# Experts in half tiles: 64-row slices, two experts side by side, the second expert's weights copied to a fixed buffer

## The chip, the cores and the metric

One core of a Trainium2 chip runs the whole program in one launch. The metric is device time in microseconds (us), the median of the runs. The kernel before takes 1213.05 us (three runs, 1210.98 to 1215.25).

## What is computed

The reference is one inference step of a one-layer hybrid decoder for 1024 prompt tokens and 8 sample tokens, width 1024, all in float32. The change touches only the last part, a mixture of experts; of the reference this matters:

```python
def grouped_moe(h, w_router, b_router, w_gate, w_up, w_down):
    scores = jax.nn.sigmoid((t @ w_router).astype(jnp.float32))
    sel = scores + b_router.astype(jnp.float32)
    ...                       # best of 4 groups of 4 experts, then the top 2 in it
    combine = ...             # (T, 16), two entries per token, which add up to 1
    hg = jnp.einsum('td,edf->tef', t, w_gate)     # e = 16 experts, d = 1024, f = 256
    hu = jnp.einsum('td,edf->tef', t, w_up)
    act = jax.nn.silu(hg) * hu * combine[..., None].astype(t.dtype)
    out = jnp.einsum('tef,efd->td', act, w_down)
```

1032 tokens go to two experts each, which makes 2064 rows. With the inputs as drawn, the reference's router gives the 16 experts 101, 121, 137, 63, 316, 175, 149, 290, 32, 128, 124, 6, 125, 131, 38 and 128 of them. The parts before it (input projection, gated DeltaNet heads, S5 channel groups, output projection) and the final norm are the same in both kernels, but for where some of their buffers lie.

## The kernel before

The program is written out by hand for five engines, with semaphores between them. Its last section routes the tokens, runs the experts and ends with the final norm.

**Routing.** While the output projection runs (L2491), each block of 128 tokens is normed (`H2`), written to DRAM as `h2_d` by SyncE (L2368) and routed. GpSimd scatters each token's number into its expert's list in DRAM (`ids_d`, L2412). When all are counted, VectorE works out a table `slot_t`, which says for each slot (a tile of rows of one expert) the expert's weight buffer, how many loads must have landed, and where its list lies, and `exp_t`, which says after how many slots each expert is done.

**Slots.** A slot is 128 rows of one expert, and each expert has at least one. The counts above give 24 slots: 1, 1, 2, 1, 3, 2, 2, 3, 1, 1, 1, 1, 1, 2, 1 and 1. Each engine runs the slots in a hardware loop over pairs of them (`pairs`, L2060), the first pair written out ahead of the loop. For slot s the engines do this:

- GpSimd loads the list of 128 token numbers (L2095) and gathers the rows of `h2_d` by it (L2102).
- TensorE transposes the rows, 8 times 128x128 (L2137). VectorE copies them out of PSUM in two halves (L2226, L2228) into `xT`.
- TensorE multiplies them with the gate and up weights, which lie beside each other as 512 columns: 8 matmuls over the 8 blocks of 128 channels (L2173). I call this gate-up.
- ScalarE makes the silu (L2209), VectorE the product with the up half (L2240).
- TensorE transposes the two halves of that (L2143), VectorE copies them out (L2249), and TensorE multiplies with the down weights, 4 matmuls of 512 columns (L2155). I call this down.
- ScalarE copies the result out of PSUM in two halves (L2194, L2195) and starts its write to `ys_d` (L2198).

TensorE's order is gate-up of slot s, activation transposes of slot s-1, row transposes of slot s+1, down of slot s-1, and so on.

**Weights.** Gate and up of one expert are 2 MB (`wgu`, which lies in `hT`, two buffers), down is 1 MB (`wdn` in `y1T`, two buffers). SyncE loads both for experts 0 and 1 ahead of the slots. For expert e from 2 on (`moe_sync`, L2081) it waits for the gate-up of the last slot of expert e-2, issues gate and up (L2009), waits for the down of that slot, issues down (L2012), and goes on to e+1. The down of a slot comes on TensorE only after the next slot's gate-up.

**After the slots.** GpSimd gathers the two result rows of each token from `ys_d` (L2273), TensorE adds them with their weights (L2291), and VectorE and ScalarE do the residual, the norm and the output. The last expert's rows must be in DRAM first (`y_done`).

The loop's frame, which the change replaces:

Of the kernel before, what the change touches and what calls it, by code (L numbers as in the profile page):

```python
# [11 lines left out]
ALU = mybir.AluOpType  # L12
# [21 lines left out]
LAGS = 8  # L34
NCH = SEQ // LAGS
# [29 lines left out]
def emit(nc, A, O, marks):  # L65
# [11 lines left out]
    with ctx:  # L77
# [7 lines left out]
        hT = sb("hT", [P, KD, T])  # L85
# [73 lines left out]
        w_ring = s2.enter_context(nc.sbuf_tensor("w_ring", [P, 2, KD, 512], F32))  # L159
# [36 lines left out]
        early = room(w_ring[:, 1].rearrange("p k n -> p (k n)"))  # L196
        crow, sq, vrow = early(9, D), early(P, D), early(117, P)
        ada_row, cP = early(P, 2, 512), early(P, KD, 32)
# [26 lines left out]
        SLOTS = 2 * T // P + EXPERTS  # L225
        ys_d = dram("ys_d", ((SLOTS + 4) * P, D))
        gate_land, conv_land, conv_out = sem("gate_land"), sem("conv_land"), sem("conv_out")
        pe, act, dve, pool = steps("s2_pe"), steps("s2_act"), steps("s2_dve"), steps("s2_pool")
        with nc.Block() as block:
            @block.sync  # L230
            def _(sp):
# [5 lines left out]
                sp.dma_start(crow[0:1, :], A["c_prompt"]).then_inc(cland, 16)  # L237
                sp.dma_start(crow[1:9, :], A["c_sample"]).then_inc(cland, 16)
# [72 lines left out]
            def _(t):  # L311
# [4 lines left out]
                for k in range(KD):  # L316
                    mm = t.transpose(ps[7][:, k * 9:k * 9 + 9], crow[:, k * P:(k + 1) * P], ident[0:9, 0:9])
# [191 lines left out]
            def _(a):  # L509
# [6 lines left out]
                act.did(a.activation(crow[:, :], crow[:, :], ACT.Silu), "silu_c")  # L516
                dve.wait(a, "clear_ss")

                def squares(i):
# [3 lines left out]
                    act.did(a.activation(sq[0:n, :], X[0:n, i, :], ACT.Square, accum_out=small[0:n, i:i + 1]), f"ss{i}")  # L523
# [483 lines left out]
        t3 = lambda name, shape: s3.enter_context(nc.sbuf_tensor(name, shape, F32))  # L1007
        egl = t3("egl", [P, NT, HEADS])
        W3 = t3("W3", [P, 3328])
        Y = t3("Y", [P, 2, HEADS, P])  # L1010
        XS = t3("XS", [P, 1024])
        Yd, Xd = t3("Yd", [P, HB, BL]), t3("Xd", [P, HB, BL])
        Sd = t3("Sd", [P, DEC, HEADS, P])
        dec = t3("dec", [P, 768])
# [9 lines left out]

        R = W3[:, 0:512].rearrange("p (h n) -> p h n", h=HEADS)
        D1 = W3[:, 512:1536].rearrange("p (b h n) -> p b h n", b=2, h=HEADS)
        egb = W3[:, 1536:2048].rearrange("p (h n) -> p h n", h=HEADS)
        knd, ud = W3[0:DEC, 2048:2560], W3[0:DEC, 2560:3072]

        r = W3[:, 0:512].rearrange("p (h n) -> p h n", h=HEADS)  # L1030
        u = W3[:, 512:1024].rearrange("p (h n) -> p h n", h=HEADS)
# [521 lines left out]
        def load_ada(sp, c):  # L1553
            sp.dma_start(ada_col[c % 2][:, :, :], w_ada[:, :, (4 + c) * 512:(5 + c) * 512]).then_inc(ada_col_land[c % 2], 16)
# [1268 lines left out]
```

## Time and profile before

| | us |
|---|---|
| runs (three) | 1215.25, 1213.05, 1210.98 |
| median | 1213.05 |
| span of the profiled execution, first to last instruction | 1212.9 |
| of it, up to the first gate-up | 843.75 |
| from there to the start of the last slot's gate-up | 285.9 |
| from there to the end of the last down | 22.75 |
| final stage | 60.5 |

The profiled execution's own time is given only as its span, which is 0.15 us under the median of the runs. In the rows, times are us from the start of the span unless marked ns. PE is TensorE's matmuls, PEld its weight loads (which overlap them), DVE is VectorE, ACT is ScalarE, POOL is GpSimd and SPq is SyncE's queue. In brackets behind a row stands how long its engine had been idle before it, and what released it. A float32 matmul shows as two records of PE and two of PEld, a transpose as one.

### The profile page before, as it was taken

To read this page: it belongs to the slowest core of one execution; us is meant where nothing else is said; L and a number is where in the kernel's file an instruction comes from. 1 tells how busy PE (TensorE), PEld (TensorE's weight loads), DVE (VectorE), ACT (ScalarE), POOL (GpSimd) and SP (SyncE) were. 2 spreads that over 40 slices of the span, in tenths; PEclk is the share of its full clock that TensorE was granted. 3 is DMA by queue.
4 is the path that set the end of the run, shared out by engine and by line. 5 is a ranking of instruction groups with operands and counts; after the bars stand their busy time and mean duration, and the time that the engine had idled before them with its cause. 6 is when DMAs were issued, how large, how long until landed. Compare 5 with 4: busy or idle time off the path is not lost. (4 is left out here: it accounts for less than half of the span.)

```text
span 1212.9 us, 15216 instructions
## 1 busy us (share of the span) xinstructions
PE 1082.3 (89%) x5092; PEld 649.4 (54%) x5093; DVE 555.6 (46%) x1290; ACT 311.3 (26%) x703; POOL 220.2 (18%) x368
## 2 busy tenths in 40 slices
PE   4899999899998899699987999983999999889876
PEld 4466666445877777578853444442444444444332
DVE  4134446774448556799614325666212121121138
ACT  6121221125113643322234233330011111111033
POOL 0100000384423443211010000222111111111060
PEclk9999999999998879799888999995999999999888
DMA  9595170120016000566373001223776756788273
GB/s 347 175 289 214 66 273 5 70 102 38 14 28 128 15 1 21 201 222 235 137 268 120 31 18 41 100 69 71 235 251 215 234 191 201 262 296 294 87 296 140
DMA packets 128048, 182.02 MB, mean 150 GB/s; under 512 B 37725, under 2 KB 81490, under 8 KB 127982
## 3 DMA queue, kind: packets, MB, share of 16 engines
q1 hardware_dynamic: 116988, 147.03, 36.5%
q0 software_dynamic: 7376, 21.59, 5.6%
q10 hardware_dynamic: 3626, 12.64, 2.6%
q8 instruction: 35, 0.57, 0.2%
q14 instruction: 23, 0.19, 0.1%
HBM read 131.69 MB, written 48.47 MB: 149 GB/s over the span
## 5 line engine op out<-in xcount | busy, mean ns | idle before, releaser
L2173 PE MATMUL bank<-hT,H 128*128 (+1 forms) x384 | 172.1, 601 | 10.0 <-DMA hT<-in_w_up 5.4
L367 PE MATMUL bank<-hT,w_ring 128*128 128x344 f32 x576 | 169.6, 456 | 3.8 <-ACT hT L551 3.8
L367 PEld LDWEIGHTS bank<-hT,w_ring 128*128 128x128 f32 x576 | 109.9, 192 | 61.9 <-issue 5.2
L2173 PEld LDWEIGHTS bank<-hT,H 128*128 128x128 f32 x384 | 72.5, 192 | 107.2 <-issue 105.2
L2240 DVE TENSOR_TENSOR H<-H,bank 128x256 f32<-128x256 f32 x24 | 10.1, 421 | 238.1 <-ACT H L2209 238.1
L452 PE MATMUL bank<-w_ring,hT 128*128 128x512 f32 x256 | 114.7, 605 | 4.3 <-ACT qkvT L579 4.3
L2491 PE MATMUL bank<-w_out,hT 128*128 128x512 f32 x256 | 116.8, 601 | 0.5 <-DVE hT L1949 0.5
L2155 PE MATMUL bank<-y1T,H 128*128 (+1 forms) x192 | 91.2, 619 | 10.7 <-DVE H L2249 7.9
L452 PEld LDWEIGHTS bank<-w_ring,hT 128*128 128x128 f32 x256 | 64.2, 255 | 50.5 <-issue 32.1
L2491 PEld LDWEIGHTS bank<-w_out,hT 128*128 128x128 f32 x256 | 46.3, 190 | 49.8 <-issue 47.2
L2155 PEld LDWEIGHTS bank<-y1T,H 128*128 128x128 f32 x192 | 35.4, 194 | 52.2 <-issue 51.8
L2209 ACT ACTIVATE H<-bank 128x256 f32<-128x256 f32 x24 | 9.2, 385 | 177.5 <-PE bank L2173 177.5
L2102 POOL DMA_INDIRECT H<-h_d,small_room x24 | 23.4, 977 | 124.9 <-DMA small_room<-ids_d 85.2
L911 DVE SCALAR_TENSOR_TENSOR qkvT<-pre,vecT,qkvT 128x1024 f32<-128x1024 f32 x36 | 46.0, 1279 | 0.0
L573 ACT ACTIVATE pre<-bank 128x344 f32<-128x344 f32 x36 | 13.9, 458 | 122.9 <-PE bank L367 122.9
L2194 ACT ACTIVATE H<-bank 128x512 f32<-128x512 f32 x24 | 14.3, 597 | 119.7 <-PE bank L2155 119.7
L2412 POOL DMA_INDIRECT ids_d<-small_room x18 | 18.1, 1004 | 133.3 <-DVE small_room L2665 119.8
L2137 PE MATMUL bank<-ident,H 128*128 128x128 f32 x200 | 26.9, 279 | 11.6 <-DMA H<-h_d,small_room 11.6
L2095 POOL DMA_DIRECT2D small_room<-ids_d x25 | 14.0, 558 | 126.6 <-issue 125.9
L2291 PE MATMUL bank<-w_out,hT 128*128 128x512 f32 (+1 forms) x56 | 27.3, 639 | 8.5 <-DMA w_out<-ys_d,pos 6.2
L904 DVE COPY tail<-pre 128x11 f32<-128x11 f32 x12 | 2.1, 173 | 71.1 <-ACT pre L573 71.1
L1894 PE MATMUL bank<-H,y1T 128*128 128x512 f32 (+1 forms) x72 | 33.5, 626 | 0.2 <-DMA H<-in_s_glu_b 0.2
(556 smaller groups left out, 1757.5 us busy)
## 6 DMA issues: line engine op xcount, KB each, us to landing
ys_d<-ZO SPq DMA_DIRECT2D x18, 1024.0 KB, 13.1
y1T<-in_w_down SPq DMA_DIRECT2D x16, 1024.0 KB, 5.5
hT<-in_w_gate SPq DMA_DIRECT2D x16, 1024.0 KB, 7.2
hT<-in_w_up SPq DMA_DIRECT2D x16, 1024.0 KB, 10.4
ys_d<-H ACTq DMA_DIRECT2D x24, 512.0 KB, 5.2
w_ring<-in_w_in SPq DMA_DIRECT2D x4, 2048.0 KB, 8.3
y1T<-in_w_ada SPq DMA_DIRECT2D x4, 2048.0 KB, 9.1
hT<-in_w_ada SPq DMA_DIRECT2D x4, 2048.0 KB, 14.2
```

The lines of the kernel that those rows point to most:

```text
L367: mm = t.matmul(ps[3 * (m % 2) + s][:, 0:SEG], w_ring[:, q % 2, k, (m % 4) * P:(m % 4 + 1) * P], hT[:, k, s * SEG:(s + 1) * SEG], start=(k ...
L452: mm = t.matmul(ps[b % 4][0:n, :], tok, w_ring[:, q % 2, k, :], start=(k == 0), stop=(k == KD - 1))
L911: dve.did(v.scalar_tensor_tensor(out=y, in0=pre[:, m % 2, i:i + SEQ], scalar=taps[i], in1=y, op0=ALU.mult, op1=ALU.add), f"conv{m}")
L1894: mm = t.matmul(ps[2 + i % 2][0:n, :], y1T[:, k, i * P:i * P + n], glu_w[:, k, :], start=(k == 0), stop=(k == 3))
L2102: g.indirect_dma_start(xin[p][:, :], None, h2_d, bass.IndirectOffsetOnAxis(ap=who[p][:, 0:1], axis=0)).then_inc(x_in[p], 16)
L2137: mm = t.transpose(ps[k // 4][:, (k % 4) * P:(k % 4 + 1) * P], xin[p][:, k * P:(k + 1) * P], ident[:, :])
L2155: mm = t.matmul(ps[5 + half_][:, :], aT[p][:, k, :], wdn[:, bass.ds(buf, 1), k, half_ * 512:(half_ + 1) * 512].rearrange("p o n -> p (o n) ...
L2173: mm = t.matmul(ps[2 + p][:, :], xT[p][:, k, :], wgu[:, bass.ds(buf, 1), k, :].rearrange("p o n -> p (o n)"), start=(k == 0), stop=(k == K ...
L2194: a.activation(yo[p][:, 0:512], ps[5][:, :], ACT.Copy).then_inc(y_half, 1)
L2291: mm = t.matmul(ps[(5, 2)[i % 2] + half_][:, :], diag[0:n, i % 2, j, :], ya[i % YA][0:n, j, half_ * 512:(half_ + 1) * 512], start=(j == 0) ...
L2412: g.indirect_dma_start(ids_d, bass.IndirectOffsetOnAxis(ap=spot[0:n, i, j:j + 1], axis=0), ids[0:n, i:i + 1], None).then_inc(scat, 16)
L2491: mm = t.matmul(ps[b][:, :], hT[:, k, i * P:(i + 1) * P], w_out[:, k, cols], start=(k == 0), stop=(k == KD - 1))
```

## The change

- A slot becomes a **tile** of two **slices** of 64 rows (`LANES = 2`, `SLICE = 64`). Each expert gets as many slices as its rows need (at least one, the first expert at least two), and consecutive slices share a tile, so a tile can hold two experts. The counts above give 2, 2, 3, 1, 5, 3, 3, 5, 1, 2, 2, 1, 2, 3, 1 and 2 slices, together 38, in 19 tiles. Tile 3 holds experts 2 and 3, tile 6 holds 4 and 5, tile 9 holds 6 and 7, tiles 12 to 14 hold 8 and 9, 9 and 10, 10 and 11, tile 17 holds 13 and 14; in the others both slices are of one expert.
- In gate-up and down each matmul becomes two, one per slice, with 64 stationary columns and its own half of the PSUM partitions, and the same 512 moving columns each from its own weights.
- The first slice's weights are addressed by a register, the second's lie in a fixed fourth buffer. Each tile copies them there, even where both slices are of one expert: of gate-up, ScalarE and VectorE copy 2048 elements per partition each, of down 1024 each.
- There are three weight buffers for loads instead of two (`BUFS = 3`). Expert 2's weights are loaded ahead of the tiles too, its down weights behind the decode rows' `h2_d` write, its gate and up weights right behind expert 1's. For expert e from 3 on SyncE waits for expert e-3.
- To make room, `hT` and the output weights lie in one tensor `hw` (a row of `hT` is no longer followed by the next), `y1T` and `Yt` in one tensor `yy`, and buffers of the earlier sections lie in pieces of `hw`.
- GpSimd waits for the loads of both slices and then signals `gu_ready` and `dn_ready`; the list of a tile is fetched by an indirect transfer.
- The loop is written out: 17 tiles always, then up to 8 more, each behind an `If`, and behind each the end of the section under another `If`.

The core of the diff:

```diff
@@ weights
-        wgu = hT[:, :, 0:SEQ].rearrange("p k (b n) -> p b k n", b=2)
-        wdn = y1T[:, :, :].rearrange("p k n -> p (k n)")[:, 0:4 * D].rearrange("p (b k n) -> p b k n", b=2, k=2)
+        BUFS = 3
+        wgu = hw[:, :, 0:(BUFS + 1) * 2 * FE].rearrange("p k (b n) -> p b k n", b=BUFS + 1)
+        wdn = yy[:, 0:(BUFS + 1) * 2 * D].rearrange("p (b k n) -> p b k n", b=BUFS + 1, k=2)
@@ the frame
+        def tiles(eng, body, tail):
+            for s in range(LEAST):
+                body(s)
+            used = eng.value_load(exp_t[0:1, EXPERTS - 1:EXPERTS], min_val=LEAST, max_val=MOST)
+            for s in range(LEAST, MOST + 1):
+                if s < MOST:
+                    with eng.If(used > s):
+                        body(s)
+                with eng.If(used == s):
+                    tail(s - 1)
@@ SyncE
         def moe_sync(sp):
             dve.wait(sp, "slots")
+            for e in range(BUFS, EXPERTS):
+                done = sp.value_load(exp_t[0:1, e - BUFS:e - BUFS + 1], min_val=1, max_val=MOST)
+                sp.wait_ge(gu_ps, done)
+                load_gate_up(sp, e)
+                sp.wait_ge(dn_ps, done)
+                load_down(sp, e)
@@ GpSimd
+            def weights(s, landed, first, unit, ready):
+                need = [g.value_load(slot_t[0:1, s, first + b:first + b + 1], ...) for b in range(BUFS)]
+                for b in range(BUFS):
+                    g.wait_ge(landed[b], need[b])
+                g.sem_inc(ready, 1)
+            def body(s):
+                rows_in(s + 1)
+                if s + 2 <= MOST:
+                    list_in(s + 2)
+                weights(s + 1, gu_in, 2, 32, gu_ready)
+                if s > 0:
+                    weights(s, dn_in, 5, 16, dn_ready)
@@ the copies (eng is ScalarE with n = 0, VectorE with n = 1)
+        def gate_up_copy(eng, copy, n, s):
+            b = second(eng, s)
...
+                eng.wait_ge(gu_ready, s)
+                eng.wait_ge(gu_ps, s)
+            copy(wgu[:, BUFS, 4 * n:4 * n + 4, :], wgu[:, bass.ds(b, 1), 4 * n:4 * n + 4, :].rearrange("p o k n -> p (o k) n")).then_inc(gu_two[n], 1)
@@ TensorE, gate-up (down likewise)
-                    for k in range(KD):
-                        mm = t.matmul(ps[2 + p][:, :], xT[p][:, k, :], wgu[:, bass.ds(buf, 1), k, :].rearrange("p o n -> p (o n)"),
-                                      start=(k == 0), stop=(k == KD - 1))
+                for k in range(KD):
+                    if k % 4 == 0:
+                        t.wait_ge(gu_two[k // 4], s + 1)
+                    for j in range(LANES):
+                        lane = slice(j * SLICE, (j + 1) * SLICE)
+                        mm = t.matmul(ps[2 + p][lane, :], xT[p][:, k, lane], wgu[:, bass.ds(bufs[j], 1), k, :].rearrange("p o n -> p (o n)"),
+                                      start=(k == 0), stop=(k == KD - 1))
@@ ScalarE
+            def body(s):
...
+                a.activation(sg[p][:, :], ps[2 + p][:, 0:FE], ACT.Silu).then_inc(silu_sb, 1)
+                gate_up_copy(a, copy, 0, s + 1)
+                if s > 0:
+                    out(s - 1)
+                down_copy(a, copy, 0, s)
@@ VectorE
+            def body(s):
...
+                    a_copy(s - 1)
+                gate_up_copy(v, v.tensor_copy, 1, s + 1)
+                x_copy(s + 1)
+                v.wait_ge(silu_sb, s + 1)
...
+                v.tensor_tensor(hh_[p][:, :], sg[p][:, :], ps[2 + p][:, FE:2 * FE], ALU.mult).then_inc(h_sb, 1)
+                down_copy(v, v.tensor_copy, 1, s)
@@ SyncE ahead of the tiles
+                    elif i == ORDER[8]:
+                        pe.wait(sp, f"mix{i}_1")
+                        load_gate_up(sp, 1)
+                        load_gate_up(sp, 2)
```

How this stands on TensorE, for one slot of the kernel before inside its loop (`hT` and `H` are weights and rows; each row of gate-up is one block of 128 channels):

```order
L2173 ISA [waits h_sb]
L2173 MATMUL bank<-hT,H 128x512
L2173 ISA
L2173 MATMUL bank<-hT,H 128x512
...
L2143 MATMUL bank<-ident,H 128x128 [waits h_sb]
L2143 MATMUL bank<-ident,H 128x128
L2133 ISA
L2137 MATMUL bank<-ident,H 128x128 [waits xT_sb,x_in1]
L2137 MATMUL bank<-ident,H 128x128 x7
```

and for one tile of the changed kernel, L2202 being gate-up and `hw` holding the weights:

```order
L2202 ISA [waits h_sb,gu_two_act,gu_ready,xT_sb]
L2202 MATMUL bank<-hw,H 64x512 x2
L2202 ISA
L2202 MATMUL bank<-hw,H 64x512 x2
L2202 ISA
...
L2185 MATMUL bank<-ident,H 128x128 [waits h_sb]
L2185 MATMUL bank<-ident,H 128x128
L2179 MATMUL bank<-ident,H 128x128 [waits xT_sb,x_in0]
L2179 MATMUL bank<-ident,H 128x128 x7
```

Each block of channels has two matmuls of 64 stationary columns in place of one of 128, and gate-up waits for the copies (`gu_two_act`, `gu_two_dve`) beside the rows. On VectorE one slot of the loop before was this:

```order
L2240 TENSOR_TENSOR H<-H,bank 128x256 [waits aT_ps]
L2248 REGISTER_ALU [waits aT_ps]
L2249 COPY H<-bank 128x256 [waits dn_ps]
L2223 REGISTER_ALU
L2226 COPY H<-bank 128x512 [waits gu_ps,xT_ps]
L2228 COPY H<-bank 128x512 [waits xT_half]
```

and one tile now is this:

```order
L2294 COPY H<-bank 128x256 [waits aT_ps]
L2146 TENSOR_LOAD slot_t
L2146 ISA x2
L2156 ISA [waits gu_ps,gu_ready]
L2156 COPY hw<-hw 128x4x512
L2286 COPY H<-bank 128x512 [waits gu_ps,xT_ps]
L2288 COPY H<-bank 128x512 [waits xT_half]
L2311 TENSOR_TENSOR H<-H,bank 128x256 [waits silu_sb]
L2146 TENSOR_LOAD slot_t
L2146 ISA x2
L2165 ISA [waits dn_ps,dn_ready]
L2165 COPY yy<-yy 128x1024
```

The copy of the transposed activations moved from behind the product to the front, the copy of the gate-up weights stands ahead of the two row copies, and the product and the copy of the down weights stand behind them.

## Rows read from the trace of the kernel before

**Rows 1.** The page: the span, and one group of instructions that runs once per slot.

```profile
span 1212.9 us, 15216 instructions
...
L2209 ACT ACTIVATE H<-bank 128x256 f32<-128x256 f32 x24 | 9.2, 385 | 177.5 <-PE bank L2173 177.5
```

**Rows 2.** Stages: us, busy (instructions) by engine, granted clock, DMA share, GB/s.

```profile
1038.50:1129.65 91.15, 82.97 (x239) 39.08 (x239) 14.35 (x28) 10.28 (x21) 10.72 (x14) 1.00 0.84 288
1129.65:1152.40 22.75, 18.29 (x46) 8.24 (x45) 2.48 (x5) 2.56 (x5) 0.00 (x0) 0.85 0.25 93
```

**Rows 3.** TensorE's timeline over one steady slot: start, us, what, count, idle before.

```profile
953.19 7.03 PE L2173 MATMUL bank<-hT,H 128*128 x16
960.05 0.38 PE L2143 MATMUL bank<-ident,H 128*128 128x128 f32 x2
960.27 1.04 PE L2137 MATMUL bank<-ident,H 128*128 128x128 f32 x8
961.57 3.69 PE L2155 MATMUL bank<-y1T,H 128*128 x8 [0.26 <-DVE H L2249]
...
965.37 7.13 PE L2173 MATMUL bank<-hT,H 128*128 x16
```

**Rows 4.** TensorE's timeline inside the output projection: the 32-column matmuls of the decode rows.

```profile
721.44 0.19 PEld L2491 LDWEIGHTS bank<-w_out,hT 128*128 128x128 f32 x1 [0.24 <-issue]
722.39 0.16 PEld L2494 LDWEIGHTS bank<-w_out,hT 128*32 128x32 f32 x8 [0.76 <-issue]
722.39 3.64 PE L2494 MATMUL bank<-w_out,hT 128*32 128x512 f32 x32
```

**Rows 5.** Groups by line: VectorE and ScalarE over 512 and 1024 elements from SBUF.

```profile
L743 DVE TENSOR_SCALAR ZO<-ZO,small 128x1024 f32<-128x1024 f32 x8 | 5.6, 749 | 0.1
L1943 DVE TENSOR_SCALAR Yt<-Yt,small 128x512 f32<-128x512 f32 x8 | 3.3, 483 | 0.1
L2316 ACT ACTIVATE hT<-X 128x1024 f32<-128x1024 f32 x8 | 8.5, 1057 | 26.7 <-DVE X L2337 26.7
```

**Rows 6.** Timeline of VectorE after a gate-up that ended at 1045.6.

```profile
1046.22 0.42 DVE L2240 TENSOR_TENSOR H<-H,bank 128x256 f32<-128x256 f32 x1 [10.36 <-ACT H L2209]
1046.56 0.42 DVE L2249 COPY H<-bank 128x256 f32<-128x256 f32 x1
1046.89 0.68 DVE L2226 COPY H<-bank 128x512 f32<-128x512 f32 x1
...
1047.61 0.69 DVE L2228 COPY H<-bank 128x512 f32<-128x512 f32 x1
```

**Rows 7.** TensorE's waits among the slots, then the timeline around one late load.

```profile
PE bank L2173 <- DMA hT<-in_w_up: 5.4, 2, 3.0
...
1038.40 0.37 SPq L2012 DMA_DIRECT2D y1T<-in_w_down  x1
...
1039.89 0.38 SPq L2009 DMA_DIRECT2D hT<-in_w_gate  x1
...
1053.83 7.13 PE L2173 MATMUL bank<-hT,H 128*128 x16 [3.02 <-DMA hT<-in_w_up]
```

**Rows 8.** Timeline from the list scatters to the second slot.

```profile
818.84 0.96 POOL L2412 DMA_INDIRECT ids_d<-small_room  x1 [0.30 <-issue]
826.42 0.60 POOL L2406 DMA_DIRECT2D small_room<-ids_d  x1 [6.63 <-DMA ids_d<-small_room]
...
840.27 1.97 PE L2137 MATMUL bank<-ident,H 128*128 128x128 f32 x8 [11.58 <-DMA H<-h_d,small_room]
843.75 9.02 PE L2173 MATMUL bank<-hT,H 128*128 128x512 f32 x16 [1.51 <-DVE H L2228]
...
855.47 7.13 PE L2173 MATMUL bank<-hT,H 128*128 x16 [1.82 <-DVE H L2228]
```

**Rows 9.** TensorE's timeline behind the loop: the last down, the final stage's first matmuls.

```profile
1146.36 6.18 PE L2155 MATMUL bank<-y1T,H 128*128 x8 [2.83 <-issue]
...
1164.40 9.11 PE L2291 MATMUL bank<-w_out,hT 128*128 128x512 f32 x16 [6.21 <-DMA w_out<-ys_d,pos]
```

More of the change, by code:

```diff
@@ L34 @@
 LAGS = 8
+LANES = 2
+SLICE = P // LANES
 NCH = SEQ // LAGS
@@ L2182, in tail @@
-            def tail(it, s):
-                act_transposes(1, s)
-                down(1, s)
-            transposes(0, 0, 0)
-            pairs(t, body, tail)
+                        for j in range(LANES):
+                            lane = slice(j * SLICE, (j + 1) * SLICE)
+                            mm = t.matmul(ps[5 + half_][lane, :], aT[s % 2][:, k, lane],
+                                          wdn[:, bass.ds(bufs[j], 1), k, half_ * 512:(half_ + 1) * 512].rearrange("p o n -> p (o n)"),
+                                          start=(k == 0), stop=(k == 1))
@@ new lines, in down, with tail @@
+                mm.then_inc(dn_ps, 1)
+            def body(s):
+                gate_up(s, buffers(s))
+                if s > 0:
+                    act_transposes(s - 1)
+                transposes(s + 1)
+                if s > 0:
+                    down(s - 1, buffers(s - 1))
+                elif s == 0:
+                    dve.wait(t, "slots")
+            def tail(s):
+                act_transposes(s)
+                down(s, buffers(s))
+            for j in range(LANES):
+                if j == 0:
+                    dve.wait(t, "el")
+                mm = t.matmul(ps[5][0:1, P + j * S2_:P + (j + 1) * S2_], ident[:, j * SLICE:j * SLICE + 1], el[:, :], start=True, stop=True)
@@ L2188, in moe_scalar, with out @@
+            pe.did(mm, "e_rows")
+            transposes(0)
+            tiles(t, body, tail)
         def moe_scalar(a):
-            def out(it, p, s):
+            def out(s):
+                p = s % 2
                 a.wait_ge(dn_ps, s + 1)
-                if not (isinstance(it, int) and it == 0):
-                    a.wait_ge(y_out[p], it * 16)
+                if s >= 2:
+                    a.wait_ge(y_out[p], 16 * (s // 2))
                 a.activation(yo[p][:, 0:512], ps[5][:, :], ACT.Copy).then_inc(y_half, 1)
@@ L2375, in _ @@
             def _(g):
+                for b in range(BUFS):
+                    g.sem_inc(gu_in[b], 1)
+                    g.sem_inc(dn_in[b], 1)
                 pool.did(g.tensor_copy(pick16[:, :], ident[:, 0:EXPERTS]))
```

500 lines of the change are left out of this document (245 added, 255 removed).

## The prediction, on record before the changed kernel ran

> **What bounds the kernel now.** I read the page first, then the windows by stage, then TensorE's timeline and waits among the slots. The span is 1212.9 us, and a group that runs once per slot counts 24 [rows 1], as the counts of rows per expert say. The first gate-up starts at 843.75 [rows 8], the last slot's at 1129.65 [rows 2], 23 steps in 285.9 us. In a steady slot TensorE has one idle time, 0.26 us ahead of down; from gate-up to gate-up it takes 965.37 - 953.19 = 12.18 us [rows 3]. So 23 steps come to 280.1, and 5.4 us of the rest are two waits for gate and up weights [rows 7]. The experts are bound by TensorE, slot by slot, and a slot costs the same however few of its 128 rows are used. In the last stretch of slots the DMA engines are busy for 0.84 of the time at 288 GB/s, TensorE for 83.0 of 91.2 us [rows 2]: the transfers are the next bound there.
>
> **What goes.** 24 slots become 19 tiles. The question is what a tile costs, and what late weights cost when each tile eats more of them.
>
> **A tile on TensorE.** Gate-up has 16 matmuls of 64 stationary columns in place of 8 of 128, with the same moving columns. The 16 records of a slot take 6.86 us from their start to the first transpose [rows 3], 0.43 us each. If the halves ran one after the other, a tile would need 32 times 0.43. The nearest row is a group of 16 matmuls with 32 stationary columns in four column groups and four different moving operands: 32 records in 3.64 us [rows 4], where one after the other they would take 13.8, so 3.8 of 4 ran at once. I take it that two halves run fully beside each other, and gate-up stays at 6.86 and down at 3.80 (961.57 to 965.37) [rows 3]. The Trainium skill (TensorE: Matmul & The Clock Gate, Part 3) gives 2.38 times for three column groups, 0.79 of the ideal. By that ratio gate-up and down would take 1.26 times as long; the trace of this kernel disagrees, with 3.8 of 4.
>
> Changing from 128 to 32 columns costs something: the weight load stands 0.95 us behind the one before it, not 0.43 [rows 4]. The load can't go beside the matmul ahead of it. Its matmul then waits some 0.25 us that it didn't before (the load of 0.16 and the gap; bounds 0 and 0.52). A tile has two such changes, out of gate-up into the transposes and back into down: 0.5 us. Against that the 0.26 us wait ahead of down goes, since VectorE now copies the transposed activations first. A tile: 6.86 + 1.26 (transposes) + 3.80 + 0.5 = 12.4 us. Bounds: 11.9 without cost for the changes, 13.0 with 0.52 each.
>
> **The copies.** VectorE handles 1024 float32 from SBUF in 749 ns and 512 in 483 [rows 5], 0.52 ns each; 2048 come to 1.28 us, 1024 to 0.75. ScalarE handles 1024 in 1057 and 256 in 385 [rows 5, 1], 0.875 ns each; 2048 come to 1.95 us, 1024 to 1.06. TensorE has 1.26 + 3.80 + 0.5 = 5.6 us between two gate-ups. In it VectorE does the activations' copy (0.42, after 0.4 of transposes), its weight copy (1.28) and the two row copies (1046.89 to 1048.30, 1.41 [rows 6]): 3.5 us. ScalarE does the silu (0.39) and its copy (1.95): 2.4. Both fit, and the down copies have a whole tile. Price 0 in the steady tile, hidden by TensorE's own 5.6 us. Even with VectorE at one element per 1.04 ns, twice the price, it is 4.8 and fits. The register loads for buffers and semaphores run on the sequencers ahead of their work, as they do now; 0.
>
> **Late weights.** The copies aren't hidden when a tile waits for its weights: then come GpSimd's signal (0.2, a guess), VectorE's copy and the row copies behind it (2.7) and a handover of 0.1, 3.0 us from landing to gate-up. Where does this happen? Before, gate of expert 10 was issued at 1039.89, as SyncE was held by the down of the slot before until 1038.4 and then needed 1.5 us, and gate-up began at 1053.83 [rows 7]: 13.9 us, less 0.2 is 13.7 from issue to both landed. Now from tile 12 on every tile needs one new expert. Let G be the start of gate-up of tile 13. Expert 11 waits for expert 8, long done, but SyncE is held by the down of tile 11, which ends at G. It issues at G + 1.5, lands at G + 15.2, gate-up of tile 14 starts at G + 18.2 and not at G + 12.4: 5.8 lost. Expert 12 is issued after the down of tile 12, at G + 13.8, and lands at G + 27.5, just in time for tile 15 (G + 30.6). Expert 13 waits for the down of tile 13, which came late with tile 14; issued at G + 32.1, it opens tile 16 at G + 48.8 and not at G + 43.0: 5.8 again. Experts 14 and 15 are issued soon after one another and are in time. So 11.6, say 12 us, where 5.4 stand now. Bounds: 0, if a load takes less than before, and 30, if five tiles wait for 5.9 each.
>
> **The start.** Four MB of weights are issued at 811 in place of two. The scatters of token numbers landed only 6.6 us after the last was issued [rows 8], and on that chain hangs the first gather, which ended TensorE's wait of 11.58 us at 840.27. With twice the bytes ahead of them I give it 3 us (0 to 7; the upper end is about the 6.6 once more). The first step from gate-up to gate-up was 11.72 (843.75 to 855.47); now VectorE copies weights behind gate-up (9.02 - 0.1, then 1.28, 1.41 and 0.3), 12.0.
>
> **The end and the rest.** Behind the last gate-up all is as before: 22.75 us to the end of the last down [rows 2], then the final stage. The new code has 11 skipped blocks there; I give it 0, as TensorE waits 6.21 us for gathered rows [rows 9] and would be late by that much before anyone notices. The moved buffers change strides, not amounts, in the earlier sections: 0, bounds -1 and +2.
>
> **Sum.** From the first gate-up before to the last tile's now: 3 + 12.0 + 17 times 12.4 (210.8) + 12 = 237.8, against 285.9. That is 48.1 less, and 1212.9 - 48.1 = 1164.8 by the profiled execution, whose span is 0.15 under the median. I forecast 1165 us.
>
> **Rivals.**
>
> *No load is late.* Three buffers and a request two tiles ahead would cover it, if SyncE's being held didn't count. Against: it counted twice before. Without the 12 us: 1153.
>
> *Weights bound the last tiles.* The stretch that moved 288 GB/s had one expert per slot like these, and DMA at 0.84 [rows 2]; a third buffer adds no bandwidth. If tiles 14 to 18 all wait 5.9, 30 in place of 12: 1183.
>
> *Skipped code.* Behind the loop TensorE stood for 2.83 us with nothing but its own sequencer to wait for [rows 9]. Now it must pass five unused tile bodies of code written out. If each costs 2.83, 14.2 less the cover of 6.2 is 8 us: 1173. The Trainium skill (Runtime: NRT & Kernel Launch, Instruction fetch mechanics) says that a taken branch to code outside the two pages held forces a fetch before execution goes on. No row here shows such a fetch by itself.
>
> *The halves don't overlap (slower).* Two column groups could do worse than four: each float32 matmul has two records that must follow one another in the same columns, and with only two groups nothing else may be ready. One after the other, the 12 blocks of gate-up and down cost 0.86 us more each, 19 times 12 times 0.86 = 196: 1361. It decides from 48.1 / 228 = 0.21 us per block: above 1.07 us for both halves, in place of 0.86, the kernel gets slower. The Trainium skill's ratio of 0.79, cited above, would give 1.09, and so 1217. For it speaks only that no row shows two groups at 512 columns; against it stand the 32 records in 3.64 us [rows 4].
>
> **How the numbers follow.** My forecast 0.60, no late load 0.09, weights bound 0.14, skipped code 0.10, halves not overlapping 0.07. The first four are faster, the last slower: faster 0.92, same 0.01, slower 0.07. Within 0.3% is what a measurement of this kernel can't tell from no change. The range takes in the first four with the bounds of a tile (17 times 0.5 down, 17 times 0.6 up) and of the start: from 1153 - 6 = 1147 to 1183 + 9 = 1192.
>
> **What would show it.** TensorE's timeline should have 19 gate-ups of about 6.9 us and starts 12.4 apart in the middle; 13 or more there means that column changes or copies cost more, 22 that the halves don't overlap. Waits in front of gate-up for copies of late weights should stand at tiles 14 and 16, some 6 us each, and nowhere before tile 12. The first gate-up should start near 847. TensorE's idle time after the last down, up to the first sum of gathered rows, should stay at 12 us; if it grows, the skipped code costs. I'm wrong if the middle step isn't within 11.9 to 13.0, or if the waits of the last seven tiles lie outside 0 to 30.

## The result, and the profile after

| | before | after |
|---|---|---|
| median, us | 1214.13 (1210.98 to 1215.25, 4 runs) | 1166.12 (1158.17 to 1167.80, 4 runs) |
| ratio, with 95% interval | 1 | 0.9594 (0.9563 to 0.9625) |
| profiled execution: span, us | 1212.9 | 1166.0 (its own time 1167.80) |
| mean granted clock of TensorE | 0.941 | 0.924 |

The changed kernel is 48 us faster, and 1165 was forecast. The spans differ by 46.9 us, and four stretches make that up:

| stretch | before | after | difference | forecast |
|---|---|---|---|---|
| start to the first gate-up | 843.75 | 849.88 | +6.1 | +3 |
| first gate-up to the last one | 285.9 | 229.9 | -56.0 | -51.1 |
| last gate-up to the end of the last down | 22.8 | 20.8 | -2.0 | 0 |
| from there to the end | 60.5 | 65.4 | +4.9 | 0 |

The total is right to 1 us. Its terms are not, and they cancelled by luck, as the rest of this document shows. The page of the changed kernel, first part and costliest groups (the columns are those of [rows 1]):

```profile
span 1166.0 us, 15446 instructions
...
L2202 PE MATMUL bank<-hw,H 128*64 (+1 forms) x608 | 141.0, 618 | 16.3 <-DVE H L2288 13.5
...
L2274 ACT ACTIVATE hw<-hw 128x2048 f32 (+1 forms) x20 | 38.2, 1911 | 39.3 <-DVE small_room L2336 18.9
...
L2156 DVE COPY hw<-hw 128x2048 f32 (+1 forms) x20 | 24.5, 1226 | 22.6 <-POOLq L2122 14.6
...
L2263 ACT ACTIVATE H<-bank 128x256 f32<-128x256 f32 x19 | 7.3, 385 | 75.1 <-PE bank L2202 75.1
```

The silu group, 24 in [rows 1], counts 19: the change does what it says. Gate-up's 608 records are 19 times 32. The weight copies took 1.23 us on VectorE and 1.91 on ScalarE, where 1.28 and 1.95 were worked out from [rows 5].

TensorE's timeline of one steady tile (start, length, line, operation, count, idle time before it), to be laid beside [rows 3]:

```profile
945.81 7.04 PE L2202 MATMUL bank<-hw,H 128*64 x32
952.78 0.44 PE L2185 MATMUL bank<-ident,H 128*128 128x128 f32 x2
953.05 1.04 PE L2179 MATMUL bank<-ident,H 128*128 128x128 f32 x8
954.02 3.65 PE L2220 MATMUL bank<-yy,H 128*64 x16
957.50 7.04 PE L2202 MATMUL bank<-hw,H 128*64 x32
```

From gate-up to the first transpose 32 records take 6.97 us. Sixteen records of 128 columns took 6.86. Two experts beside each other thus cost what one cost. The tile takes 957.50 - 945.81 = 11.69 us, where 12.4 was forecast and a slot had 12.18. The idle 0.26 us ahead of down is gone. [Rows 3] show one of two kinds of slot, which took turns in the kernel before: in the other, down waited 0.43 us, and the slot took 12.18 as well.

The stretch between the first gate-up and the last is 12.33 us for the first tile, 17 times 11.69 (198.8), and three lumps on top of these: 1.75 in the second tile, 8.6 in tile 14 and its follower, 8.4 in tile 16 and its. TensorE's waits from 800 to 1110 us (engine, line, what it waited for, total, times, longest):

```profile
PE bank L2202 <- DVE H L2288: 13.5, 3, 6.2
...
PE bank L2392 <- issue: 7.0, 1, 7.0
...
PE bank L2220 <- ACT yy L2274: 3.3, 1, 3.3
PE bank L2202 <- ACT hw L2274: 2.8, 1, 2.8
```

The first is mostly the two waits of tiles 14 and 16. The second and third come up below. The fourth is the second tile waiting for the copies of its weights, of which ScalarE's ended last. It lies in the first tile's 12.33 us; the 1.75 us of the second tile are its gate-up, 8.79 us long in place of 7.04. The timeline at the late loads, TensorE's rows first, then SyncE's and VectorE's that fall between them:

```profile
1004.28 7.04 PE L2202 MATMUL bank<-hw,H 128*64 x32
...
1022.34 9.32 PE L2202 MATMUL bank<-hw,H 128*64 x32 [6.20 <-DVE H L2288]
...
1036.31 7.04 PE L2202 MATMUL bank<-hw,H 128*64 x32
...
1054.00 8.85 PE L2202 MATMUL bank<-hw,H 128*64 x32 [5.83 <-DVE H L2288]
...
1004.49 0.37 SPq L2022 DMA_DIRECT2D yy<-in_w_down  x1
1005.46 0.37 SPq L2019 DMA_DIRECT2D hw<-in_w_gate  x1
...
1019.64 1.23 DVE L2156 COPY hw<-hw 128x2048 f32 x1 [7.50 <-POOLq L2122]
```

Tiles 14 and 16 waited 6.20 and 5.83 us, with 5.8 forecast for the same two tiles. As in [rows 7], SyncE issued a down only when gate-up of tile 13 had begun, and gate and up of the next expert 1 us later. The copy began 14.2 us after that, and gate-up 2.7 us after the copy: 13.7 + 0.2 and 2.7 + 0.1 in the prediction. What it left out stands in the windows of four stretches (stretch: length, busy time of PE, PEld, DVE, ACT, POOL with counts, granted clock, DMA share, GB/s):

```profile
875.65:1004.28 128.63, 128.63 (x641) 48.79 (x639) 43.57 (x66) 48.84 (x55) 21.84 (x20) 1.00 0.78 258
1004.28:1022.34 18.06, 11.86 (x61) 4.30 (x57) 3.78 (x6) 5.25 (x7) 0.25 (x1) 0.94 0.96 317
1022.34:1036.31 13.97, 13.97 (x58) 5.06 (x60) 4.06 (x7) 3.51 (x4) 4.53 (x4) 0.84 0.57 190
1036.31:1054.00 17.69, 11.86 (x60) 4.30 (x57) 3.77 (x6) 5.24 (x7) 0.24 (x1) 0.91 0.95 318
```

In eleven steady tiles TensorE is busy all the time at a granted clock of 1.00 (the level of 2.4 GHz). Behind the two long waits the clock falls, to a mean of 0.84 in tile 14: part of it ran at 1.2 GHz, gate-up took 9.32 us in place of 7.04, and the tile 13.97 in place of 11.69. Tile 16 took 14.09. So these two waits of 6 us cost 8.5 each. Behind shorter ones it varied: the wait of 2.79 us was followed by a gate-up of 8.79 us here, and by one of 7.09 in the kernel with the edits joined.

### The profile page after: what moved, and what is told of

The parts are those of the page before. It is cut to its first block and busy times, and to the rows that moved or that the text cites. A ratio compares the mean times of both kernels' runs of the same rounds, so it can differ in the third digit from the quotient of the medians.

```text
span 1166.0 us, 15446 instructions
## 1 busy us (share of the span) xinstructions
PE 1033.9 (89%) x5382; PEld 604.8 (52%) x5382; DVE 581.7 (50%) x1309; ACT 361.8 (31%) x726; POOL 227.6 (20%) x363
## 5 line engine op out<-in xcount | busy, mean ns | idle before, releaser
L371 PE MATMUL bank<-hw 128*128 128x344 f32 x576 | 169.7, 456 | 3.8 <-ACT hw L555 3.8
L2202 PE MATMUL bank<-hw,H 128*64 (+1 forms) x608 | 141.0, 618 | 16.3 <-DVE H L2288 13.5
L371 PEld LDWEIGHTS bank<-hw 128*128 128x128 f32 x576 | 109.8, 192 | 62.0 <-issue 5.4
L456 PE MATMUL bank<-hw 128*128 128x512 f32 x256 | 114.7, 605 | 4.3 <-ACT qkvT L583 4.3
L2620 PE MATMUL bank<-hw 128*128 128x512 f32 x256 | 116.8, 601 | 0.4 <-DVE hw L1954 0.4
L2202 PEld LDWEIGHTS bank<-hw,H 128*64 128x64 f32 x608 | 45.2, 143 | 108.5 <-issue 106.6
L456 PEld LDWEIGHTS bank<-hw 128*128 128x128 f32 x256 | 64.2, 254 | 50.5 <-issue 32.1
L2220 PE MATMUL bank<-yy,H 128*64 128x512 f32 (+1 forms) x304 | 71.0, 610 | 3.3 <-ACT yy L2274 3.3
L2620 PEld LDWEIGHTS bank<-hw 128*128 128x128 f32 x256 | 46.3, 190 | 49.7 <-issue 47.2
L2274 ACT ACTIVATE hw<-hw 128x2048 f32 (+1 forms) x20 | 38.2, 1911 | 39.3 <-DVE small_room L2336 18.9
L2405 PE MATMUL bank<-hw 128*128 128x512 f32 (+1 forms) x72 | 34.7, 630 | 3.5 <-ACT hw L2416 3.5
L2156 DVE COPY hw<-hw 128x2048 f32 (+1 forms) x20 | 24.5, 1226 | 22.6 <-POOLq L2122 14.6
L1899 PE MATMUL bank<-H,yy 128*128 128x512 f32 (+1 forms) x72 | 33.1, 620 | 0.8 <-DMA H<-in_s_glu_b 0.8
## 6 DMA issues: line engine op xcount, KB each, us to landing
hw<-in_w_ada SPq DMA_DIRECT2D x8, 1024.0 KB, 12.1
```

The source lines that it names most:

```text
L371: mm = t.matmul(ps[3 * (m % 2) + s][:, 0:SEG], w_ring[:, q % 2, k, (m % 4) * P:(m % 4 + 1) * P], hT[:, k, s * SEG:(s + 1) * SEG], start=(k ...
L456: mm = t.matmul(ps[b % 4][0:n, :], tok, w_ring[:, q % 2, k, :], start=(k == 0), stop=(k == KD - 1))
L1899: mm = t.matmul(ps[2 + i % 2][0:n, :], y1T[:, k, i * P:i * P + n], glu_w[:, k, :], start=(k == 0), stop=(k == 3))
L2156: copy(wgu[:, BUFS, 4 * n:4 * n + 4, :], wgu[:, bass.ds(b, 1), 4 * n:4 * n + 4, :].rearrange("p o k n -> p (o k) n")).then_inc(gu_two[n], 1)
L2202: mm = t.matmul(ps[2 + p][lane, :], xT[p][:, k, lane], wgu[:, bass.ds(bufs[j], 1), k, :].rearrange("p o n -> p (o n)"), start=(k == 0), st ...
L2220: mm = t.matmul(ps[5 + half_][lane, :], aT[s % 2][:, k, lane], wdn[:, bass.ds(bufs[j], 1), k, half_ * 512:(half_ + 1) * 512].rearrange("p ...
```

## The experiments

Each kernel is the changed kernel with the edit shown. Ratios are to the kernel before, run on the same chip beside it; its median there was 1211.70, 1214.76 or 1214.42 us. Two of these kernels may have run on different chips, and that stands behind a comparison of their medians.

### SyncE asks for gate and up first

```diff
-    sp.wait_ge(gu_ps, done)   # expert e, then its down:
-    load_gate_up(sp, e)
-    sp.wait_ge(dn_ps, done)
-    load_down(sp, e)
+    sp.wait_ge(gu_ps, done)   # expert e, then the down of e - 1:
+    load_gate_up(sp, e)
+    sp.wait_ge(dn_ps, held)
+    load_down(sp, e - 1)
```

> SyncE requests gate and up of expert e+1 before it waits for the down that frees expert e's down buffer; nothing else changes. Theory, requests are held: gate and up of expert 11 are asked for at the end of tile 12's gate-up, 5.9 us earlier than at 1005.46, that of expert 13 likewise. The waits of 6.20 and 5.83 us at tiles 14 and 16 go or fall under 1 us, and with them the slow gate-ups behind them (9.3 and 8.9 us against 7.0). The steps from tile 13 to tile 17, 63.8 us now, come near 4 times 11.7 = 46.8, and the kernel gains 14 to 17 us: about 1150. Rival, bandwidth: the stretches with the two waits moved 317 and 318 GB/s with DMA at 0.96 and 0.95, a tile that needs a new expert moves about 4.2 MB, and that takes 12.7 to 13.2 us however early it is asked for. Then waits of 1 to 2 us spread over tiles 13 to 18, and the gain is 6 us or less.

It took 1152.45 us, ratio 0.9496 (0.9468 to 0.9523), which is 13.7 less than the changed kernel by the medians, just short of the 14 to 17 expected. The windows of its tiles 13 and 14, and then 15:

```profile
1005.39:1028.78 23.39, 23.39 (x119) 8.87 (x116) 8.11 (x12) 8.88 (x10) 1.89 (x2) 1.00 1.02 350
1028.78:1044.48 15.70, 13.54 (x60) 5.20 (x58) 4.05 (x6) 4.44 (x5) 3.95 (x4) 0.89 1.06 375
```

The four steps that took 63.8 us took 50.8, and TensorE no longer waits for weights. The transfers ran at 350 to 375 GB/s in these windows. So the waits came from SyncE being held by a down, and not from bandwidth: the rival by which weights bound the last tiles falls. The 4.0 us missing from 46.8 are one step of 15.70, and a new wait. On GpSimd and TensorE:

```profile
1028.88 1.12 POOL L2119 DMA_INDIRECT H<-h_d,small_room  x1 [11.02 <-DMA yy<-in_w_down]
...
1038.34 1.82 PE L2183 MATMUL bank<-ident,H 128*128 128x128 f32 x8 [2.16 <-DMA H<-h_d,small_room]
```

GpSimd stood for 11.02 us in its wait for a tile's down weights, and the gather of a later tile's rows, which needs nothing of them, was queued behind. The gathered rows came late.

### The end: conditions nested

Before, each engine meets the blocks of tiles that aren't used one after another. Here the next tile's condition stands inside the one before it.

```diff
-for s in range(LEAST, MOST + 1):
-    if s < MOST:
-        with eng.If(used > s):
-            body(s)
-    with eng.If(used == s):
-        tail(s - 1)
+def rest(s):
+    with eng.If(used == s):
+        tail(s - 1)
+    if s < MOST:
+        with eng.If(used > s):
+            body(s)
+            rest(s + 1)
+rest(LEAST)
```

> Each conditional tile stands inside the condition of the one before it, so that an engine leaves all unused code by one branch. Theory, skipped code: TensorE's idle time of 7.02 us after the last down, which only its own sequencer explains, falls under 3 us, the first sum of gathered rows starts 12 to 13 us after the last down's end in place of 17.0, as in the kernel before (12.0), and the kernel gains 4 to 5 us. Rival, the clock: the final stage starts late because its small transposes run at the lower clock (10.0 us against 5.8); then the idle time falls but the sum still starts 15 us or more after the last down. Rival, gathers: the rows arrive late anyway, no gain.

It took 1158.56 us, ratio 0.9545 (0.9513 to 0.9577). TensorE's timeline behind the last down, first of the changed kernel, then of this one:

```profile
1095.33 5.24 PE L2220 MATMUL bank<-yy,H 128*64 x16 [3.31 <-ACT yy L2274]
1107.58 0.80 PE L2392 MATMUL bank<-ident,modT 128*128 128x128 f32 x2 [7.02 <-issue]
...
1117.60 2.67 PE L2405 MATMUL bank<-hw 128*128 128x512 f32 x4
```

```profile
1093.02 3.65 PE L2222 MATMUL bank<-yy,H 128*64 x16 [3.31 <-ACT yy L2276]
1098.61 0.49 PE L2394 MATMUL bank<-ident,modT 128*128 128x128 f32 x2 [1.94 <-issue]
...
1108.82 10.13 PE L2407 MATMUL bank<-hw 128*128 128x512 f32 x16 [4.27 <-DMA hw<-ys_d,pos]
```

The idle time in which nothing but its own sequencer held TensorE goes from 7.02 to 1.94 us. From the end of the last down to the first sum it takes 12.15 us, where the changed kernel had 17.0 and the kernel before 11.9 (1164.40 less 1152.54, [rows 9]). That is the +4.9 of the end. In the changed kernel TensorE didn't wait for the gathered rows at all. GpSimd issued their first gather at 1106.02; in the nested kernel they released TensorE 6.7 us after that issue, so here I estimate that they were there by 1112.7, 5 us before the sum. Part of the 17.0 is the clock: the transposes in that stretch ran 10.0 us in place of 5.8, behind the idle time. Not all of the 5 us comes back: the nested kernel waits 4.27 us for the rows, and its first sums then take 10.13 us, where the changed kernel's took 7.82. From the end of the last down to the end of the span it is 61.6 us against 65.4. The other 3.9 of the 7.7 us between the spans lie ahead of that, and nothing shows that they are the edit's. The medians differ by 7.6 us, where I expected 4 to 5. The Trainium skill (Runtime: NRT & Kernel Launch, Instruction fetch mechanics) says that a taken branch to code outside the two pages held has to fetch it first. These rows agree as far as they go, and the idle time is 5.1 us shorter when one branch passes all the unused blocks. No row shows the fetch by itself, and a fixed cost for each condition would fit them too.

### The start: the third expert's weights later

Two kernels put off the load of the third expert's gate and up.

```diff
-    load_gate_up(sp, 2)
+                load_gate_up(sp, 2)          # the first: behind h2_d's last write
+                sp.wait_ge(x_in[0], 16)      # the second: once the first
+                load_gate_up(sp, 2)          # tile's rows have landed
```

> Gate and up weights of expert 2 are requested behind the last write of h2_d, not right behind expert 1's. Theory, the scatters and the list queue behind 2 MB more: GpSimd's wait for the scatters goes from 10.01 back to about 6.6 us, the wait for the list from 4.60 to 2.9, and the first gate-up starts near 845, 5 us earlier than at 849.88; tile 2 doesn't wait. Rival: the new table of slices or the copy of the first weights made the start late; then it stays above 848.

It took 1166.35 us, ratio 0.9619 (0.9586 to 0.9651), the same as the changed kernel. GpSimd's timeline, first of the changed kernel, then of this one:

```profile
821.65 0.96 POOL L2541 DMA_INDIRECT ids_d<-small_room  x1 [0.30 <-issue]
832.62 0.60 POOL L2535 DMA_DIRECT2D small_room<-ids_d  x1 [10.01 <-DMA ids_d<-small_room]
837.82 0.99 POOL L2541 DMA_INDIRECT ids_d<-small_room  x1 [4.60 <-DMA small_room<-ids_d]
...
840.38 1.00 POOL L2137 DMA_INDIRECT H<-h_d,small_room  x1 [0.30 <-issue]
```

```profile
829.53 0.60 POOL L2535 DMA_DIRECT2D small_room<-ids_d  x1 [6.95 <-DVE small_room L2828]
832.33 0.99 POOL L2541 DMA_INDIRECT ids_d<-small_room  x1 [2.20 <-DMA small_room<-ids_d]
...
834.90 1.00 POOL L2137 DMA_INDIRECT H<-h_d,small_room  x1 [0.30 <-issue]
```

The scatters and the list come 5.5 us sooner, and with that the gather is issued sooner. But from the gather's issue to the transposes of its rows it now takes 10.7 us (834.90 to 845.56), where the changed kernel took 6.0 (840.38 to 846.41), and the first gate-up starts at 849.04. The late transfer, issued at 831.19, now stood in front of the gather. So the wait moved from the scatters to the gather, and my expectation, a first gate-up near 845, was a miss. The second kernel puts the load behind both:

> SyncE asks for gate and up of expert 2 only when the first gathered rows have landed. In the run with the load behind the last write of h2_d the scatters came 3.1 us sooner, but the gather of the first rows then took 9.9 us. Theory, whatever lies ahead of a transfer on that chain delays it: with nothing ahead of either, the first gate-up starts at 843 to 845, and the kernel gains 5 us (1161). Rival: the gather is slow for another reason, the first gate-up stays above 848.

Its first gate-up started at 846.16, 3.7 us sooner, and it took 1161.79 us, ratio 0.9571 (0.9538 to 0.9604). From the last scatter ahead of the list to the first gate-up it takes 24.3 us (821.88 to 846.16). With the load ahead of the scatters it is 28.2 (821.65 to 849.88) in the changed kernel and 28.4 to 32.0 in the five others of that order; with it behind the rows it is 24.2 to 24.4 in all four. The kernel before had 24.9 (818.84 to 843.75, [rows 8]). So the load's whole cost comes back. The 2.4 us that the first gate-up is still late, and more, lie ahead of the scatters: 821.88 against 818.84.

### The copies made small

Each weight copy handles 64 elements per partition. It leaves out most of the second slice's weights, so that slice is computed with others.

```diff
-copy(wgu[:, BUFS, 4 * n:4 * n + 4, :], wgu[:, b, 4 * n:4 * n + 4, :])
+copy(wgu[:, BUFS, 4 * n:4 * n + 1, 0:64], wgu[:, b, 4 * n:4 * n + 1, 0:64])
```

> Leaves out nearly all of the copies of the second slice's weights: of gate-up and of down each engine copies 64 elements per partition in place of 2048 and 1024, so the second slice is computed with stale weights. Theory, the copies are hidden in a steady tile: the step stays at 11.69 us. They show only where nothing covers them: the step into tile 1 loses about 1 us, the steps into tiles 14 and 16 lose 1.1 us each (VectorE's 1.23 us copy), the last down's wait of 3.31 us for the copy loses 1 us; 4 us in all. Rival, the copies slow something in every tile (SBUF access of the matmuls or of the transfers): the step falls below 11.5 us, or the loads land sooner than 14.15 us after the request.

It took 1162.26 us, ratio 0.9585 (0.9549 to 0.9621). TensorE's timeline, a steady tile and then the two late ones:

```profile
920.49 7.04 PE L2202 MATMUL bank<-hw,H 128*64 x32
...
932.18 7.04 PE L2202 MATMUL bank<-hw,H 128*64 x32
...
1017.38 8.78 PE L2202 MATMUL bank<-hw,H 128*64 x32 [3.17 <-DVE H L2288]
...
1047.92 8.78 PE L2202 MATMUL bank<-hw,H 128*64 x32 [3.15 <-DVE H L2288]
```

The steady tile stays at 11.69: there the copies are hidden. Where weights are late they aren't: the first tile takes 11.03 in place of 12.33, and VectorE's copy takes 0.20 us in place of 1.23. The late waits are some 3 us shorter, where I expected 1.1. The rest isn't shown to be the copies' doing. At tile 14 the copy began 12.2 us after the request in place of 14.2, the loads having landed sooner; but the two kernels with nested conditions and with the late third load, whose copies and late requests are those of the changed kernel, waited 4.27 and 6.20 us there, the first with 12.3 us from request to copy. So such a difference comes between kernels without this edit too. At tile 16, 1.27 us of the wait went to the gathered rows just before. Little of the gain reaches the end, because the last tiles wait for gathered rows (steps of 14.97 and 14.26, the first of them also with the slow gate-up of tile 16):

```profile
1058.38 1.09 PE L2179 MATMUL bank<-ident,H 128*128 128x128 f32 x8 [1.31 <-DMA H<-h_d,small_room]
...
1072.64 1.09 PE L2179 MATMUL bank<-ident,H 128*128 128x128 f32 x8 [2.35 <-DMA H<-h_d,small_room]
```

### Whole tiles in the new frame

One expert of up to 128 rows per tile, as before, in the changed kernel's frame: three buffers, unrolled code, VectorE's new order. There are 24 tiles and no copies.

```diff
-LANES = 2
+LANES = 1
-return first, BUFS
+return (first,)
-MOST = -(-((2 * T + EXPERTS * (SLICE - 1)) // SLICE + LANES - 1) // LANES)
+MOST = 26
```

> The changed kernel with whole tiles: LANES = 1, so 24 tiles of 128 rows of one expert, no second slice, no copies; three buffers, the loop written out (with at most 26 tiles in place of the general bound) and GpSimd's signals stay. It tells what the slices alone bring. Theory, the number of tiles is the gain: 23 steps of about 12.0 us, no late load (with one expert a tile and three buffers SyncE asks two tiles ahead), so 276 us from the first to the last gate-up against 229.9 with slices and 285.9 before, a first gate-up near 850, and about 1207 in all: the frame and the buffers bring 5 to 10 us of the change's 48, the slices the rest. Rival, three buffers and the written-out loop bring most of it: under 1190.

It took 1187.95 us, ratio 0.9791 (0.9761 to 0.9821). I had expected 1207, so that was a miss, and the rival that named a time under 1190 came true. By the medians it is 27 of the 48 us, by the ratios 2.1 of 4.1 per cent: about half of the gain isn't from the slices. TensorE's timeline of a tile:

```profile
971.42 7.03 PE L2200 MATMUL bank<-hw,H 128*128 x16
978.28 0.38 PE L2185 MATMUL bank<-ident,H 128*128 128x128 f32 x2
978.50 1.04 PE L2179 MATMUL bank<-ident,H 128*128 128x128 f32 x8
979.37 3.60 PE L2216 MATMUL bank<-yy,H 128*128 x8
```

A tile takes 11.39 us, and none waits for late weights. Three things follow. Slices cost 11.69 - 11.39 = 0.30 us per tile, 0.5 being forecast. The frame with VectorE's new order brings the slot from 12.18 to 11.39, of which I had counted 0.26, and the third buffer takes away the two waits of 5.4 us in all. And between the first and the last gate-up the slices bring 262.0 - 229.9 = 32.1 us; in this pair of profiles the changed kernel gives back 3.7 of that before the first gate-up and 9.8 from the start of the last one to the end of the span. This kernel has only one unused tile to pass there, and TensorE shows no idle time of its own sequencer. One more kernel puts VectorE's old order back into this one:

```diff
-a_copy(s - 1)
-x_copy(s + 1)
 v.tensor_tensor(hh_[p], sg[p], ps[2 + p], ALU.mult)
+a_copy(s - 1)
+x_copy(s + 1)
```

> The kernel with whole tiles, and VectorE's order as it was before the change: the product first, then the copy of the transposed activations, then the row copies. With VectorE's new order its step is 11.39 us against 12.18 of the kernel before, though both have the same matmuls. Theory, the order: in the kernel before, down stood 0.43 us late, idle and with its first weight load uncovered, as the copy came behind the product. Then the step goes to 11.8 or more, and the wait ahead of down by VectorE's L2249 counterpart comes back. Rival, the written-out loop: the gaps came from register loads and branches, the step stays at 11.4.

A single run gave 1209.02 us. Its tile on TensorE:

```profile
938.64 7.03 PE L2200 MATMUL bank<-hw,H 128*128 x16
945.50 0.38 PE L2185 MATMUL bank<-ident,H 128*128 128x128 f32 x2
945.72 1.04 PE L2179 MATMUL bank<-ident,H 128*128 128x128 f32 x8
947.02 3.70 PE L2216 MATMUL bank<-yy,H 128*128 x8 [0.26 <-DVE H L2287]
950.55 7.03 PE L2200 MATMUL bank<-hw,H 128*128 x16
```

The tile takes 11.91 us, 0.52 more, though the idle time is 0.26. From the start of the transposes to the start of down it is 1.30 us against 0.87: beside the idle time down's first weight load is no longer covered. The other 0.09 lies between the start of down and the next gate-up. The remaining 12.18 - 11.91 = 0.27 is left for the rest of the frame. In [rows 3] it stands between down and the next gate-up, 3.80 us where this kernel has 3.53. That the loop becoming written-out code took it away is likely, but no kernel here changes that alone. The span is 22.7 us above that of the kernel without this edit; between the first and the last gate-up it is 14.5, and the rest, 6.6 of it ahead of the first gate-up, isn't explained by this edit.

### The edits joined

Three edits together: SyncE's order, nested conditions, the third expert's load behind the rows.

> Three edits together: SyncE's order of the load requests, the nested conditions, and expert 2's gate and up behind the first rows. If their gains add up, 13 (steps), 5 (end) and 5 (start) give about 1143; if they get in each other's way, because the transfers left out at the start come back later, 1150.

It took 1142.81 us, ratio 0.9412 (0.9379 to 0.9444): the gains add up, as 1143 said. Two steps still took 13.6 us, for gathered rows. The next kernel also lets GpSimd issue the next gather before it waits for down weights:

```diff
-weights(s + 1, gu_in, 2, 32, gu_ready)
-if s > 0:
-    weights(s, dn_in, 5, 16, dn_ready)
+if s > 1:
+    weights(s - 1, dn_in, 5, 16, dn_ready)
+weights(s + 1, gu_in, 2, 32, gu_ready)
```

> The joined kernel, and GpSimd waits for a tile's down weights only after it has issued the gather of the tile after next. With SyncE's new order TensorE's step into tile 16 had grown to 15.7 us because GpSimd stood 11.0 us at down weights before it issued that tile's gather. Theory, the gather was held: that step comes to 12 to 13 us, 3 us less. Rival, bandwidth: that stretch moved 350 to 375 GB/s with DMA at 1.0; then the wait goes to the weights, and the time stays within 1 us of the joined kernel's.

The window over four of its late tiles:

```profile
1010.21:1057.08 46.87, 46.87 (x235) 17.70 (x233) 15.91 (x24) 17.75 (x20) 9.01 (x8) 1.00 1.01 365
```

All steps from the second tile on are 11.69 to 11.75 us, at a granted clock of 1.00, in this window with 365 GB/s. The held gather was the cause of the two longer steps. By the medians, 1141.46 against 1142.81, ratio 0.9402 (0.9376 to 0.9428), the two kernels can't be told apart. Last, ScalarE copies the down weights before it writes out the tile before:

```diff
-if s > 0:
-    out(s - 1)
 down_copy(a, copy, 0, s)
+if s > 0:
+    out(s - 1)
```

> The joined kernel with GpSimd's order, and ScalarE copies its half of the down weights before it copies the result of the tile before out of PSUM. The last down waited 3.31 us for that copy, behind two copies of 0.6 us and the start of a write. Theory: that wait falls to 1 or 2 us, nothing else moves, a gain of about 2 us. Rival: the result of the tile before leaves PSUM 1.5 us later, and with it its write, which the final stage waits for in the last tile: no gain.

```profile
1071.72 3.65 PE L2226 MATMUL bank<-yy,H 128*64 x16 [2.06 <-ACT H L2259]
```

The wait ahead of the last down falls from 3.31 to 2.06 us. It took 1138.97 us, ratio 0.9382 (0.9345 to 0.9419). It is the lowest median of all: 75 us below the kernel before, 27 below the changed one. The wait is shorter by 1.25 us, just short of what I expected; that this last edit by itself makes the kernel faster the ratios, 0.9382 and 0.9402 with intervals that overlap, don't show.

## Why the prediction was right, and where not

**That halves run beside each other** was right, and carried the forecast. 32 records in 6.97 us, against 6.86 for 16 of full width, is all but 2 of 2; the row with four groups [rows 4] spoke truly. The rival without overlap falls, and with it the 2.38 for three groups of the Trainium skill (TensorE: Matmul & The Clock Gate, Part 3) as a guide to two: the measurement decides.

**The tile, 12.4 us**, was the term most mis-sized: it measured 11.69, 12.1 us over 17 tiles. The step that failed is "against that the 0.26 us wait ahead of down goes". The reorder was worth 0.52, as the experiment with the old order shows. I read the idle time and missed that [rows 3] also show down starting 1.30 after the transposes' start, with a weight load in the open. The step that took down at the 3.80 of [rows 3] failed too: it now takes 3.48, and 0.27 of the difference came with the rest of the frame, probably the written-out code, which I had put at nothing. The slices with their two changes of column width cost 0.30 in all, not 0.5. Even the lower bound of 11.9 was too high.

**Late weights, 12 us**: place and mechanism were right, tiles 14 and 16, SyncE held by a down. The size was 17. The step "5.8 lost" has no term for what comes after: the clock granted falls behind a wait, and the next tile loses 2.3. [Rows 7] didn't show that, as gate-up there took 7.13 us behind a wait of 3.02. The final stage of the kernel before did. Behind 6.21 us of waiting its first group of 16 matmuls took 9.11 us [rows 9], and the next one, of the same size, 7.13:

```profile
1174.58 7.13 PE L2291 MATMUL bank<-w_out,hT 128*128 128x512 f32 x16 [1.07 <-ACT hT L2302]
```

The first two tiles cost 2.1 us more than forecast, 1.75 of it the second's slow gate-up.

**The start, 3 us**, measured 6.1, near the upper bound of 7. What it priced came out right: from the last scatter to the first gate-up it took 28.2 us in place of 24.9, which is 3.3 more (the wait for the scatters 10.01 in place of 6.63, then the list 1.7 later still, the gather 1.8 quicker). The other 2.8 lie ahead of the last scatter, in the sections for which the step "The moved buffers change strides, not amounts" had 0 and at most 2. Why is open; in the other kernels with the changed frame that scatter starts anywhere from 816.89 to 822.25.

**The end, 0**, measured +4.9 (and 2.0 less ahead of it). The step "I give it 0, as TensorE waits 6.21 us for gathered rows" failed. Passing the unused blocks outlasted that cover. The rival on skipped code, with 8 us and a chance of 0.10, was the right mechanism. It didn't exclude the forecast's other terms, and I had treated it as if it did.

**The copies, 0**, was right in the steady tile, as was the 2.7 us from the start of VectorE's copy to gate-up.

**The sum** came out within 1 us of the median because 12 us too much on the tile stood against 5 too little at the late loads, 3 at the start and 5 at the end; the 2.1 too little for the first two tiles and the 2.0 too much for the last down cancel too. That is luck. And the forecast put nearly the whole gain on 24 becoming 19. By the medians the slices bring some 22 us of the 48, the frame and VectorE's order some 27. A forecast that hits with such terms isn't one to trust at the next size. The range isn't what its own bounds give either: 1153 less 17 times 0.5 less 3 is 1141.5, not 1147, and 1183 with 17 times 0.6 and 4 is 1197, not 1192.

What stays open: what delays the scatters by 3 us, which part of the frame brings the 0.27 us, what in passing the unused blocks takes the time, and whether the second slice's weights could be used in place. No kernel here was run for any of these.

## What to carry to other kernels

Price an idle time by the start of the work before it and of the work behind it, not by the idle time the row prints; uncovered weight loads and a lower clock come on top, and here made 0.26 into 0.52 and 6 into 8.5. Where one queue serves several streams in order, ask at each wait what stands behind it and needs nothing of it: of the edits here that leave nothing out and gave the changed kernel something, all but the nested conditions were only such a reorder. And count code that is skipped: a chain of unused blocks ahead of a stage can outlast the wait that was to cover it, as it did here.

## What the hardware showed that I hadn't expected

- Two column groups of 64 with 512 moving columns in float32 overlap wholly (6.97 against 6.86 us). With four groups of 32 it had been 3.8 of 4 [rows 4].
- With transfers at 350 and 365 GB/s and a DMA share around 1.0, TensorE ran on at a granted clock of 1.00 and tiles kept 11.7 us. The lower clocks among the late tiles all stand behind a wait: 0.84 behind 6.20 us. But not every wait has one: gate-up took 7.13 us behind 3.02 [rows 7], and 8.78 behind 3.17 with the small copies.
- The third expert's transfer delays the small indirect ones behind it: the wait for the scatters was 10.0 to 12.4 us in the six kernels with it ahead and 5.4 to 7.1 in the five that show this wait without it, and from the gather's issue to the first work on its rows it took 10.7 with the transfer just ahead and 6.0 to 7.8 otherwise.
